# Where the weight parts stand between the modulation units of a diffusion layer's opening, and 24 spare transposes on TensorE

## The reference

```python
sh1, sc1, gt1, sh2, sc2, gt2 = adaln(c, w_mod[l], b_mod[l])       # silu(c) @ w_mod + b_mod
csh1, csc1, ... = adaln(c_ctx, w_mod[l], b_mod[l])
hx = modulate(rms_norm(x, g_mix[l]), sh1, sc1)                     # xn * (1 + scale) + shift
hc = modulate(rms_norm(ctx, g_mix[l]), csh1, csc1)
... = jnp.split(hx @ w_in[l], N_IN_SLICES, axis=-1)                # eight slices of 512
... = jnp.split(hc @ w_in[l], N_IN_SLICES, axis=-1)
# four token mixers (pooling, spatial gating, RG-LRU, attention),
# gated merge (w_gate, w_branch), w_out, residual,
# adaLN again, SwiGLU (w_ffn_gate, w_ffn_up, w_ffn_down), final RMSNorm
```

## Time and profile before

| what | before |
|---|---|
| median of three executions | 1638.8 us |
| the profiled execution: time, span | 1638.07 us, 1636.4 us |
| TensorE busy, share of the span | 1607.0 us, 98% |
| VectorE, ScalarE, GpSimd busy | 1098.0, 726.4, 159.6 us |
| read from HBM | 386.35 MB, mean over the span 238 GB/s |
| the opening, to TensorE's last of 160 parts | about 158 us |

### The profile page before, as it was taken

One profiled execution on the slowest core, in us unless ns is written; L12 is line 12 of the kernel. 1 busy time (PEld: TensorE's weight loads), 2 busy tenths in 40 slices (PEclk: granted clock), 3 DMA queues, 4 the chain that ended last, 5 costly groups with the idle time before them and its releaser, 6 DMA issues.

```text
span 1636.4 us, 22699 instructions
## 1 busy us (share of the span) xinstructions
PE 1607.0 (98%) x7899; PEld 1322.7 (81%) x7899; DVE 1098.0 (67%) x1263; ACT 726.4 (44%) x812; POOL 159.6 (10%) x296
## 2 busy tenths in 40 slices
PE   6999999999999999999999999999999999999998
PEld 4678798987788888888787888888888888888876
DVE  4333556878888888878795576867755555555577
ACT  5333234468744444444445544443444444434434
POOL 1002111000022122123010010101100000000000
PEclk9999999999999999999999999999999999999999
DMA  9998746645589899899585677878776666666654
GB/s 345 356 357 243 243 146 203 222 144 158 190 298 326 276 308 329 280 342 342 208 294 157 180 237 243 279 233 267 253 254 192 187 190 192 192 192 187 187 169 139
DMA packets 200545, 390.28 MB, mean 238 GB/s; under 512 B 14400, under 2 KB 47408, under 8 KB 199584
## 3 DMA queue, kind: packets, MB, share of 16 engines
q1 hardware_dynamic: 176960, 312.51, 59.4%
q0 software_dynamic: 23312, 76.79, 14.0%
q10 hardware_dynamic: 208, 0.11, 0.0%
HBM read 386.35 MB, written 3.01 MB: 238 GB/s over the span
## 4 chain that ended last, share of the span: by engine, by line
PE 93%; DMA 3%; DVE 1%; ACT 1%; SPq 1%; issue 1%; POOL 0%; DVEq 0%; POOLq 0%; ACTq 0%
PE ps L1414 25%; PE ps L1416 25%; PE ps L1415 25%; PE ps L1386 4%; PE ps L1387 4%; PE ps L1388 4%; DMA BR<-in_w_mod 2%; PE ps L1382 2%; PE ps L1467 1%; DMA MR<-in_w_mod 1%; DVE LO L788 1%; PE ps L1578 0%; PE ps L1565 0%; PE ps L1604 0%; PE ps L1603 0%
## 5 line engine op out<-in xcount | busy, mean ns | idle before, releaser
L788 DVE TENSOR_TENSOR LO<-RAW,HI 128x1024 fp32r<-128x1024 f32 x519 | 632.8, 1223 | 403.8 <-ACT HI L447 402.4
L447 ACT ACTIVATE HI<-RAW 128x1024 fp32r<-128x1024 f32 x519 | 548.5, 1060 | 759.8 <-PE ps L1416 631.3
L1414 PE MATMUL ps<-HI,H 128*128 128x512 f32 x1840 | 721.9, 392 | 0.7 <-DVE LO L788 0.4
L1416 PE MATMUL ps<-HI,H 128*128 128x512 f32 x1840 | 716.4, 389 | 0.0
L1415 PE MATMUL ps<-LO,H 128*128 128x512 f32 x1840 | 716.0, 389 | 0.0
L1414 PEld LDWEIGHTS ps<-HI,H 128*128 128x128 f32 x1840 | 345.4, 188 | 74.7 <-issue 2.2
L1415 PEld LDWEIGHTS ps<-LO,H 128*128 128x128 f32 x1840 | 345.5, 188 | 72.4 <-issue 1.9
L1416 PEld LDWEIGHTS ps<-HI,H 128*128 128x128 f32 x1840 | 345.4, 188 | 72.4
L409 POOL DMA_DIRECT2D BR<-in_w_mod x224 | 120.4, 538 | 766.4 <-DVE BR L900 305.8
L900 DVE SCALAR_TENSOR_TENSOR BR<-BR,SCF 128x512 f32<-128x512 f32 (+1 forms) x210 | 156.8, 747 | 12.6 <-DMA BR<-in_w_mod 10.9
L1386 PE MATMUL ps<-H,HI 128*128 128x256 f32 (+1 forms) x384 | 125.6, 327 | 0.1
(11 more groups left out here) (257 smaller groups left out, 749.9 us busy)
## 6 DMA issues: line engine op xcount, KB each, us to landing
RAW<-in_w_gate SPq DMA_DIRECT2D x128, 512.0 KB, 4.7
BR<-in_w_mod POOLq DMA_DIRECT2D x224, 256.0 KB, 4.6
RAW<-in_w_ffn_gate SPq DMA_DIRECT2D x88, 512.0 KB, 3.7
RAW<-in_w_ffn_up SPq DMA_DIRECT2D x88, 512.0 KB, 3.7
RAW<-in_w_ffn_down SPq DMA_DIRECT2D x88, 512.0 KB, 3.6
RAW<-in_w_in SPq DMA_DIRECT2D x64, 512.0 KB, 5.3
BR<-in_w_mod SPq DMA_DIRECT2D x50, 512.0 KB, 9.4
RAW<-in_w_branch SPq DMA_DIRECT2D x32, 512.0 KB, 5.4
```

The costliest lines, as they stand in the source:

```text
L447: act.activation(HI[:, j % RING, :], RAW[:, j % RING, :], ACT.Copy).then_inc(hi_done, 1)
L788: tt(LO[:, j % RING, :], RAW[:, j % RING, :], HI[:, j % RING, :], ALU.subtract).then_inc(lo_done, 1)
L1414: mm(o, xh, wh, start=first and t == 0, stop=False, skip_group_check=True)
L1416: i = mm(o, xl, wh, start=False, stop=last and t == 1, skip_group_check=True)
```

## The change

The diff has three parts. Each row of DEAL gets a fifth number and others for the first four. `deal` is now called ahead of its unit and once more, with the fifth number, ahead of the turn. And behind the turn of chunk 0 TensorE issues 24 transposes of the identity into an unused stretch of bank 5 that nobody reads.

```diff
-DEAL = (None, (6, 4, 6, 5), (0, 7, 0, 8), (0, 10, 0, 8), (0, 10, 0, 8), (0, 15, 0, 10), (0, 13, 0, 10), (0, 8, 0, 4))
+DEAL = (None, (8, 0, 8, 4, 2), (0, 4, 12, 0, 2), (0, 2, 11, 0, 3), (0, 2, 11, 0, 2), (0, 5, 13, 0, 2), (0, 4, 9, 0, 3), (0, 6, 12, 0, 3))
@@
             mod1_turn(0)
+            for _ in range(24):
+                turn(ps[:, 5, 2 * P:3 * P], IDENT)
             for ch in range(1, CHUNKS):
                 for i in range(4):
+                    deal(DEAL[ch][i])
                     mod_unit(ch, i)
-                    deal(DEAL[ch][i])
+                deal(DEAL[ch][4])
                 mod1_turn(ch)
```

## The result

The changed kernel takes 1646.66 us (median of six, 1644.44 to 1649.12), the kernel before 1638.72 us (median of six, 1638.46 to 1640.72): ratio 1.0046, 95% interval 1.0036 to 1.0057. It is slower by 7.9 us. The forecast was slower, 1643.6 us, with a range of 1640.9 to 1646.0: the way was right, the size too small, and the time lies 0.7 us outside the range. The profiled execution took 1649.12 us (span 1647.4), the longest of the six. In the experiments one execution of the kernel before (2317.85 us) and one of e4 (2028.31 us) had a granted clock of 0.66 and 0.75 over the whole run; the ratios leave both out.

A forecast was written before the change was run, and what follows sets the result against it. TensorE's matmul stream was taken to bound the kernel, with 7.2 us to win in the opening. The median of before plus 3.1 us gave 1641.9, plus 1.7 for one clock fall 1643.6 us; eight-in-ten range 1640.9 to 1646.0.

The forecast's parts named there:

- The start: Behind chunk 0's turn: transposes until 31.7 us, first part at 32.0 instead of 33.13, at the full clock.
- The rule that the full clock does not engage for transpose mode: Rival at the opening: transposes do not hold the clock, first parts run slow, 1.7 us; with one fall 1645.3; chance 0.05.
- The way to h: From the first matmul behind a chunk's last unit, through ScalarE and VectorE, to the next h: 5.15 us.
- the timetable: TensorE's opening blocks at their prices: four new waits, 7.1 us, for h and a copy; chunk 4's turn at 98.7.
- The sum: Opening: chunk 4's turn +1.4, parts done +0.7, broken-up blocks in chunks 5 to 7 +1.0; in all +3.1 us.
- The way to h is mostly hidden: Rival on the waits for h: ScalarE and VectorE overlap more, 1.5 us off each wait, about 1638.1; chance 0.10.
- the rival for a faster kernel: Landings were the real limit: no part waits for h, clock never falls, 1636.2 down to 1635.0 us; chance 0.07.
- The clock: Behind the 2.9 and 2.55 us waits: zero to two falls, 0 to 3.4 us; one taken, 1.7 us.
- Both are followed by a fall: Rival on the clock: both long waits for h bring a slow stretch, 1645.3 us; chance 0.15.
- nothing else moved after 160 us: Sign in the profile after: behind the opening's 160 parts nothing changes.

The follow-up runs named there:

- e4: The kernel before with 50 spare transposes behind the last of the 160 parts, a pure delay: 1644.32 us, ratio 1.0028 against the kernel before.
- e2: The kernel before, with its own DEAL and loop, plus the 24 transposes behind chunk 0's turn: 1639.3 us, ratio 0.9996 against the kernel before.
- e1: The changed kernel without the 24 transposes, so the new deals alone: 1648.76 us, ratio 1.0048 against the kernel before.
- e3: The changed kernel with 22 and 19 spare transposes ahead of pieces 5 and 7, in the long waits for h: 1641.56 us, ratio 1.0013 against the kernel before.
- e6: The changed kernel with BETWEEN emptied, so pieces 3, 5 and 7 are halved ahead of the row's copy: 1640.71 us, ratio 1.0011 against the kernel before.
- e5: The changed kernel with only another DEAL table, leaving more parts between last units and h's consumers: 1637.32 us, ratio 0.9994 against the kernel before.
- e8: The changed kernel with BETWEEN emptied and a further DEAL table: 1638.47 us, ratio 0.9996 against the kernel before.
- e7: The changed kernel run again unchanged, for a second trace: 1644.12 us.
- e9: The changed kernel with a third other DEAL table and BETWEEN as before: 1638.88 us, ratio 1.0001 against the kernel before.
- e10: The changed kernel run again unchanged, for a third trace: 1648.00 us.

## Why the prediction was right in direction and short in size

- **The start.** Right: transposes to 31.3 (2.82 us for 24, priced at 2.98), first part at 31.86 (32.0 forecast), full clock. In the old order they are worth nothing (e2); in the new one they save a fall that nothing behind it would swallow (e1). The rule that the full clock does not engage for transpose mode (the Trainium skill, "TensorE: Matmul & The Clock Gate", Part 4) is contradicted here: in e3 22 of them stood where otherwise there was a wait, and 19 in the next, and the clock was 1.00 throughout.
- **The way to h and the timetable.** The way was right, 5.15 us forecast and 5.1 measured, and so were the waits: 0.85, 2.9, 2.55 and 0.83 forecast, 0.62, 2.91, 2.55 and 0.78 measured; turn of chunk 2 at 64.2, measured 64.32. Landing waits went, as forecast. The sum was 0.7 us too small all the same: +3.1 us without a fall, 3.8 measured (e3). What stands behind the turn of chunk 4 was right (+1.7 forecast, 62.77 for 61.09 us measured, +1.7); ahead of it the forecast had +1.4 and e3 shows +2.1. Of these 0.7 us some 0.3 are there by the turn of chunk 2, and 0.3 come between the second long wait and the turn of chunk 4 (14.69 us for the 14.35 from 84.35 to 98.7). e6 (a link taken out) and e5 (the way put under parts) move the waits as this account says, and the rival "The way to h is mostly hidden" falls. In the rival for a faster kernel, landings were to bind at chunk 4 if no part waited for h; e8, without such a wait, meets its landing only at 139 us and gains nothing.
- **The clock.** This is the step that failed: "I take one" fall, at 1.7 us. The four traces show one, two, two, and two of which one was twice as long: 6.8 us of half clock on the mean, which costs 2.8 us (1.3 to 4.3), 1.1 more than the term. The two falls I had kept as the rival "Both are followed by a fall" (1645.3) are the common case, and a stretch of 6.8 us I had not in the account at all, though nothing in one trace of before excluded it; e4 has such a stretch in the old opening. The price of 1.7 us for a fall was a little high where it begins within the wait (1.3 in e7). The two errors went opposite ways.
- **Behind the opening.** I had put this at nothing ("nothing else moved after 160 us"), and here a second term was short. 3.8 (order) + 2.8 (clock) make 6.6 of the 7.9 us; about 1.3 stay. In the traces the stretch behind the parts is 1.4 us longer on the mean (1481.7 against 1480.3). TensorE's waits there for VectorE's L1095 and L788 are 0.5 to 3.0 us in the changed kernel's traces and 0.4 and 1.5 in those of before; with these waits and the first trace's 1.7 us of half clock taken off, the six give 1479.3 to 1479.9. So most of it is waits for VectorE that change from execution to execution, and the first trace, with the clock falling behind one, has the largest share. The shift alone does not bring them: e4, shifted by 5.4 us, has 0.2 us for L1095, e2 without a shift 1.4, e3 none and e9 1.0. Whether the changed kernel meets them more often than the one before, four traces against two don't settle. The opening's shift in one trace foretells a run's median only to this accuracy: over the eight other kernels (e1 to e6, e8, e9) the time differs from it by -1.6 (e3) to +1.1 us (e6), and by +1.4 for the changed kernel. That e3 comes out 5.5 us nearer to the kernel before, where its opening wins 2.8, lies within that scatter and stays open.

The forecast was 3.1 us short: 1.1 by the clock, 0.7 by the timetable and about 1.3 behind the opening. The direction was not luck, since the four waits came where and as long as they were forecast, and moved when their cause was moved (e5, e6).

## What to carry to other kernels

Before moving filler work ahead of a short unit that other engines turn around, follow the whole way from that unit back to its consumer (here TensorE, ScalarE, VectorE, ScalarE, VectorE, 5.1 us) and keep that much independent work behind the unit; a wait for a landing that goes is no gain if a wait for this way takes its place. A wait on TensorE of the size of these (2.55 to 3.14 us; ten of the eleven in the traces of the changed kernel and e1 had half clock around or behind them) is to be priced with the slow stretches that may follow it, on the mean and at the most, not at the one length that a single trace shows. And a cost is only worth removing where nothing behind it waits anyway: the slow stretch of the old opening cost nothing.

## What the runs showed of the hardware that was not expected

- The same wait in the same program is followed by half clock of 0, 3.4 or 6.8 us: behind the wait of 2.91 us none in e7, 3.4 us in the first trace, 6.8 us in e10. Waits of 1.6 us were followed by none (e6, twice), and of three near 1.8 us one was (the merge of the first trace, 1.80) and two were not (e8 at 139.41 us, and one of 1.8 us for L788 in e1).
- Transposes of a 128 x 128 identity that nobody reads keep the clock up: 22 in 2.62 us, 50 in 5.62 us, no fall near them (e3, e4).
- A transpose in a long unbroken row costs 0.108 us (5.4 us for 50), less than the 0.124 us read from rows of 16.
